# Gate-output units placed among the scores, numerators and norms of the exponential-gate mixer

## The chip, the cores and the metric

The kernel runs on one core of one Trainium2 chip. The metric is the device time of one execution in microseconds (us), the median over several runs. Engines: TensorE (PE; PEld is its weight load), VectorE (DVE), ScalarE (ACT), GpSimd (POOL); SyncE (SP) only issues DMAs.

## The reference

256 tokens of width 1024 go through four layers of a first block and one layer of a second. A first-block layer is a feed-forward (half added), a mixer (HGRN, the exponential-gate mixer, sliding-window attention, HGRN), a second feed-forward and a gated addition. Only layer 1's mixer, `mlstm_mixer`, is touched: four heads, queries and keys of 128, values of 256. It runs in chunks in the reference; the kernel computes the same in closed form over all 256 tokens:

```python
q, k, v, og = jnp.split(x @ w_qkvo, [dqk_all, 2 * dqk_all, 2 * dqk_all + D_MODEL], axis=-1)
...
scores = jnp.einsum('bhtk,bhsk->bhts', q_, k_) * w_intra
num = w_inter[..., None] * jnp.einsum('bhtk,bhkv->bhtv', q_, C) + jnp.einsum('bhts,bhsv->bhtv', scores, v_)
den = w_inter * jnp.einsum('bhtk,bhk->bht', q_, n) + jnp.sum(scores, axis=-1)
h = num / jnp.maximum(jnp.abs(den), jnp.exp(-m_t))[..., None]
...
h = rmsnorm(from_chunks(h), norm_g.reshape(ML_HEADS, ML_DV))
h = h.reshape(B, T, D_MODEL).astype(x.dtype) * jax.nn.sigmoid(og)
return h @ w_out
```

## The kernel before

All weights come as units of 1 MB (128 partitions x 2048 floats). Each unit passes four hands, in the order in which the phases consume the units: SyncE loads it into one of four `raw` buffers, ScalarE's `high` casts it to the coarse part `w_hi`, VectorE's `low` forms the rest, `w_lo`, and TensorE multiplies both with the two parts of the operand in 48 matmuls (`project`, `project_tokens`). There are three buffers of `w_hi` and `w_lo`, so `high(m)` waits until TensorE has finished unit m-3 (`weights_used`). Every engine has one program in a fixed order that is written by hand; semaphores hold it where another engine isn't ready. What stands behind a waiting instruction on its engine waits too.

The exponential-gate mixer (`ml`) has 16 units, called u0 to u15 here: u0 to u3 queries and keys, u4 to u7 values, u8 to u11 the output gate `og`, u12 to u15 the output projection (`w_out`). Before, TensorE does u0 to u7; then the gate columns and rows of heads (`cols`, `bcast`), the scores of four heads, the guard rows, for each head its numerators and its denominator, the square sums of the four heads (two blocks of 256 columns each, L1119 and L1120); then u8 to u11, and u12 to u15. VectorE in the meantime forms the arguments of the weights (L2323, L2324), masks them and multiplies them with the scores (L2328 to L2331), copies the numerators out of PSUM (L2335), forms the norm (L2339 to L2344), scales the heads with it (L2349), and then per gate unit, in `tail`: scale (L1919), low part of the operand (L2087), weights, product (L2097). ScalarE has exponentials, squares, logarithm and, in `gates_out`, per gate unit the sigmoid (L1507) and the coarse cast of the operand (L1509). The operand of u12 has four pairs of chunks, and `w_out` waits for each pair by itself (`mo_ready`), the fourth ahead of the last quarter of u12.

`ring` says how many PSUM banks the projections rotate over: 4 or 2; a unit waits until VectorE has read the bank's last content (`bank_read`). `besides` puts a block of other matmuls ahead of the given place within a unit. A place is one eighth of the unit: six matmuls. The HGRN mixers use both.

## Time and profile before

| | us |
|---|---|
| median of 3 runs | 2505.98 |
| lowest and highest | 2505.77, 2507.32 |
| profiled execution, first to last instruction | 2505.3 |
| TensorE busy in it | 2485.4 |
| VectorE busy in it | 1823.0 |
| ScalarE busy in it | 1294.7 |

The page of the profile describes one execution. The share of busy time of TensorE is 99%, but a matmul counts as busy while it waits for the array or runs at a lower clock, and the ends of matmuls are modelled: busy does not mean fast. The granted clock is given as a share of 2.4 GHz; 0.50 is 1.2 GHz. The mixer that is changed is passed once.

### The profile page before, as it was taken

Reading aid. Unit: us, or ns where it says so; the run is one execution under the profiler, and the core shown is the slowest. Engines: PE = TensorE matmul, PEld = TensorE weight load, DVE = VectorE, ACT = ScalarE, POOL = GpSimd, SP = SyncE. Lnnn points to the kernel's source line nnn. Section 1 sums busy time; section 2 is a strip of 40 time slices with the busy share of each in tenths; the row PEclk is TensorE's granted clock in tenths of the full one; section 3 lists DMA queues with packets and bytes.
Section 4 is the critical chain, followed back from the end, with each engine's and each line's share of the span. In section 5 each row is a group of like instructions: output and inputs, shape, how many; then the busy total and the mean of one; then the engine's idle time right before and its main releaser. Section 6 shows DMA issues by size and latency. Waiting matters only on the chain.

```text
span 2505.3 us, 41816 instructions
## 1 busy us (share of the span) xinstructions
PE 2485.4 (99%) x17552; PEld 2278.0 (91%) x17552; DVE 1823.0 (73%) x2203; ACT 1294.7 (52%) x1476; POOL 29.3 (1%) x62
## 2 busy tenths in 40 slices
PE   9999999999999999999999999999999999999999
PEld 8889998898898988988888889888999889999999
DVE  7857678677856777678567876785867868788755
ACT  5545365455534565465466554654535555444643
POOL 0000000000000000000000000000000000011000
PEclk9999999999999999999999999999999999999999
DMA  7554345554544355545543554455424554445352
GB/s 268 200 202 178 110 151 191 202 184 169 201 176 161 141 180 193 194 169 189 201 148 123 186 203 183 171 199 202 170 101 175 199 202 168 169 144 173 139 194 85
DMA packets 62270, 438.04 MB, mean 175 GB/s; under 512 B 7536, under 2 KB 7664, under 8 KB 10128
## 3 DMA queue, kind: packets, MB, share of 16 engines
q1 hardware_dynamic: 59472, 426.95, 47.1%
q0 software_dynamic: 2624, 8.52, 1.1%
q8 instruction: 139, 2.28, 0.4%
q14 instruction: 35, 0.29, 0.0%
HBM read 431.25 MB, written 1.05 MB: 173 GB/s over the span
## 4 chain that ended last, share of the span: by engine, by line
PE 92%; DVE 4%; ACT 2%; issue 1%; DMA 0%; SPq 0%; DVEq 0%; ACTq 0%
PE ps L756 19%; PE ps L838 13%; PE ps L851 12%; PE ps L869 11%; PE ps L840 7%; PE ps L857 6%; PE ps L774 6%; PE ps L870 5%; PE ps L790 2%; PE ps L872 1%; PE ps L873 1%; PE ps L874 1%; ACT w_hi L1395 1%; DVE w_lo L1857 1%; PE ps L938 1%
## 5 line engine op out<-in xcount | busy, mean ns | idle before, releaser
L1857 DVE TENSOR_TENSOR w_lo<-raw,w_hi 128x2048 fp32r<-128x2048 f32 x404 | 924.5, 2291 | 284.5 <-ACT w_hi L1395 275.5
L1395 ACT CAST w_hi<-raw 128x2048 fp32r<-128x2048 f32 x404 | 770.5, 1908 | 530.1 <-PE ps L870 214.3
L756 PE MATMUL ps<-right,w_hi 128*128 128x256 f32 x2112 | 391.3, 285 | 0.1
L756 PEld LDWEIGHTS ps<-right,w_hi 128*128 128x128 f32 x2112 | 332.2, 192 | 3.2 <-issue 1.7
L756 PE MATMUL ps<-right,w_lo 128*128 128x256 f32 x1056 | 298.7, 283 | 0.0
L869 PE MATMUL ps<-hidden,w_hi 128*128 128x512 f32 x768 | 269.3, 393 | 0.0
L838 PE MATMUL ps<-left,w_hi 128*128 128x512 f32 x736 | 256.7, 395 | 1.8 <-DVE left L1913 1.8
L838 PE MATMUL ps<-right,w_hi 128*128 128x512 f32 x736 | 256.7, 395 | 0.2 <-DVE right L2035 0.2
L1938 DVE TENSOR_TENSOR scratch<-ps,scratch 128x512 f32<-128x512 f32 x176 | 121.7, 691 | 155.7 <-ACT scratch L1431 155.7
L870 PE MATMUL ps<-hidden,w_lo 128*128 128x256 f32 x768 | 214.3, 279 | 0.0
L1448 ACT CAST hidden<-scratch 128x256 fp32r<-128x256 f32 x128 | 52.0, 406 | 300.8 <-DVE scratch L1946 300.8
L840 PE MATMUL ps<-right,w_lo 128*128 128x256 f32 x736 | 204.2, 278 | 0.0
L840 PE MATMUL ps<-left,w_lo 128*128 128x256 f32 x736 | 204.2, 278 | 0.0
L756 PEld LDWEIGHTS ps<-right,w_lo 128*128 128x128 f32 x1056 | 202.5, 192 | 0.3
L756 PE MATMUL ps<-left,w_hi 128*128 128x256 f32 x992 | 184.4, 285 | 0.1
L869 PEld LDWEIGHTS ps<-hidden,w_hi 128*128 128x128 f32 x768 | 143.9, 187 | 34.4
L838 PEld LDWEIGHTS ps<-left,w_hi 128*128 128x128 f32 x736 | 138.0, 188 | 34.6 <-issue 2.4
L838 PEld LDWEIGHTS ps<-right,w_hi 128*128 128x128 f32 x736 | 138.1, 188 | 32.8 <-DVE right L2035 0.8
L851 PE MATMUL ps<-left,w_hi 128*128 128x512 f32 x672 | 160.7, 391 | 0.0
L851 PE MATMUL ps<-right,w_hi 128*128 128x512 f32 x672 | 160.7, 391 | 0.0
L756 PEld LDWEIGHTS ps<-left,w_hi 128*128 128x128 f32 x992 | 156.1, 192 | 1.0 <-DVE w_lo L1857 0.3
L851 PEld LDWEIGHTS ps<-left,w_hi 128*128 128x128 f32 x672 | 123.6, 188 | 24.1
(356 smaller groups left out, 4499.2 us busy)
## 6 DMA issues: line engine op xcount, KB each, us to landing
raw<-weights_dram SPq DMA_DIRECT2D x404, 1024.0 KB, 4.8
scratch<-scratch POOLq DMA_DIRECT2D x48, 64.0 KB, 1.9
...
```

The costliest lines, as they stand in the source:

```text
L756: last = nc.tensor.matmul(bank(e, ring)[:, half * T:(half + 1) * T], l, r, start=(place == 0 and j == 0 and half == 0), stop=(place == KC ...
L774: last = nc.tensor.matmul(o[:, b * T:(b + 1) * T], l, r, start=(k == 0 and j == 0), stop=(k == KC - 1 and j == 2))
L838: nc.tensor.matmul(o, w_hi[:, w, wc], both(XG[2][:, k]), start=(k == 0), stop=False, skip_group_check=True)
L840: last = nc.tensor.matmul(o[:, T:2 * T], w_lo[:, w, wc], XG[0][:, k, :], start=False, stop=(k == KC - 1), skip_group_check=True)
L851: nc.tensor.matmul(ps[:, up_bank(i, j) + half, :], w_hi[:, w, wc], both(XG[2][:, k]), start=(k == 0), stop=False, skip_group_check=True)
L857: last = nc.tensor.matmul(ps[:, up_bank(i, j) + half, T:2 * T], w_lo[:, w, wc], XG[0][:, k, :], start=False, stop=(k == KC - 1), skip_grou ...
L869: nc.tensor.matmul(o, w_hi[:, w, wc], both(a), start=start, stop=False, skip_group_check=True)
L870: return nc.tensor.matmul(o[:, T:2 * T], w_lo[:, w, wc], a[:, 0], start=False, stop=True, skip_group_check=True)
L1395: nc.scalar.copy(w_hi[:, m % SPLIT, :], raw[:, m % RAW, :]).then_inc(weights_hi, 1)
L1448: nc.scalar.copy(hidden_parts(i, j)[:, 0], FFN_H[:, j % 2]).then_inc(hidden_hi, 1)
L1857: V.tensor_tensor(w_lo[:, m % SPLIT, :], raw[:, m % RAW, :], w_hi[:, m % SPLIT, :].bitcast(F32), ALU.subtract).then_inc(weights_split, 1)
L1938: V.tensor_tensor(FFN_T[j % 2], up_pair(i, j)[:, :, 0:T], FFN_SMALL, ALU.add).then_inc(bank_read, 1)
```

## The change

On TensorE the units u7 to u11 are no longer bare. Columns and rows stand ahead of place 1 of u7 and the scores ahead of place 4; numerators of heads 0 and 1 within u8; guards, the numerators of heads 2 and 3 and all denominators within u9; the square sums within u10. u4 to u11 rotate over two PSUM banks, since the others hold the blocks (`score_bank`, banks 2 and 3 for numerators). The two squared blocks of a head are added by VectorE (`sum_squares`, into `ML_SS`), and TensorE's square sums are two matmuls of 512 columns in place of eight of 256. VectorE masks a head's weights with one instruction in place of two. The code of `gates_out` and `tail` is gone, and the order on ScalarE and VectorE is written out: gates 0 to 2 are scaled as their units end, their sigmoids, products, casts and low parts stand behind the norm, each kind for all three; the fourth gate follows behind the weights of u13. Nothing else in the program is moved.

```diff
@@ -518,6 +518,7 @@
         ML_DEN = chunks(5 * UNIT + 1024, 4)
         ML_ROWS = chunks(6 * UNIT, 8)
         ML_T = chunks(0, KC)
+        ML_SS = chunks(14336, 4)
...
+        def score_bank(h):
+
+            return (ps[:, 2], ps[:, 3], ps[:, 4, P:512], ps[:, 5])[h][:, 0:384]
...
-                for u in range(4, 8):
-                    project_tokens(n0 + u, e0 + u, XG)
...
-                pe.wait_ge(m["ucol"], 1)
-                pe.wait_ge(m["arg"], ML_HEADS)
-                for h in range(ML_HEADS):
-                    last = nc.tensor.matmul(ps[:, 6 + h // 2, (h % 2) * T:(h % 2 + 1) * T], selector(h),
-                                            ML_ROWS[0:4, 7, :], start=True, stop=True)
-                last.then_inc(m["guard"], 1)
-                for h in range(ML_HEADS):
+
...
+                def guards():
+                    pe.wait_ge(m["ucol"], 1)
+                    pe.wait_ge(m["arg"], ML_HEADS)
+                    for h in range(ML_HEADS):
+                        last = nc.tensor.matmul(ps[:, 6 + h // 2, (h % 2) * T:(h % 2 + 1) * T], selector(h),
+                                                ML_ROWS[0:4, 7, :], start=True, stop=True)
+                    last.then_inc(m["guard"], 1)
+
+                def numerators(h):
                     pe.wait_ge(m["w"], h + 1)
+                    if h >= 2:
+                        pe.wait_ge(m["h"], h - 1)
                     w0, w1 = ML_W[:, h, 0:T], ML_W[:, h, T:T + P]
                     for d in range(2):
                         v = ML_V[:, :, h * ML_DV + d * P:h * ML_DV + (d + 1) * P]
-                        nc.tensor.matmul(ps[:, h, d * T:(d + 1) * T], v[:, 0], w0, start=True, stop=False,
+                        nc.tensor.matmul(ps[:, 2 + h % 2, d * T:(d + 1) * T], v[:, 0], w0, start=True, stop=False,
                                          skip_group_check=True)
-                        last = nc.tensor.matmul(ps[:, h, d * T + P:(d + 1) * T], v[:, 1], w1, start=False, stop=True,
-                                                skip_group_check=True)
+                        last = nc.tensor.matmul(ps[:, 2 + h % 2, d * T + P:(d + 1) * T], v[:, 1], w1, start=False,
+                                                stop=True, skip_group_check=True)
                     last.then_inc(m["num"], 1)
...
-                pe.wait_ge(m["gexp"], 1)
-                for h in range(ML_HEADS):
...
+                def denominators(p):
+                    pe.wait_ge(m["w"], 3 + p)
...
+                def pair_of_heads(p):
+                    numerators(2 + p)
+                    denominators(p)
+
+                def square_sums():
+                    pe.wait_ge(m["gexp"], 1)
+                    for p in range(2):
+                        pe.wait_ge(m["ss"], p + 1)
+                        nc.tensor.matmul(ps[:, 6 + p, :], ones, ML_SS[:, 2 * p:2 * p + 2].rearrange("p c t -> p (c t)"),
+                                         start=True, stop=True).then_inc(m["sums"], 1)
+                for u in range(4, 7):
+                    project_tokens(n0 + u, e0 + u, XG, ring=2)
+                project_tokens(n0 + 7, e0 + 7, XG, ring=2, besides={1: columns_and_rows, 4: scores})
+                project(n0 + 8, e0 + 8, XG, ring=2, besides={2: lambda: numerators(0), 4: lambda: numerators(1)})
+                project(n0 + 9, e0 + 9, XG, ring=2,
+                        besides={0: guards, 1: lambda: pair_of_heads(0), 3: lambda: pair_of_heads(1)})
+                project(n0 + 10, e0 + 10, XG, ring=2, besides={1: square_sums})
+                project(n0 + 11, e0 + 11, XG, ring=2)
                 pe.wait_ge(m["h"], ML_HEADS)
-                for u in range(8, 12):
-                    project(n0 + u, e0 + u, XG)
                 w_out(i, n0 + 12, e0 + 12)
...
                 for h in range(ML_HEADS):
                     act.wait_ge(m["arg"], h + 1)
                     nc.scalar.activation(ML_W[:, h], ML_W[:, h], ACT.Exp).then_inc(m["exp"], 1)
+                high(n0 + 7 + SPLIT)
+                square(0)
+                square(1)
+                high(n0 + 8 + SPLIT)
                 act.wait_ge(m["guard"], 1)
                 nc.scalar.activation(ML_GUARD.rearrange("p c t -> p (c t)"),
                                      ps[:, 6:8, :].rearrange("p b t -> p (b t)"), ACT.Exp).then_inc(m["gexp"], 1)
...
+                square(2)
+                square(3)
...
+                high(n0 + 9 + SPLIT)
                 act.wait_ge(m["nrm"], 2)
                 link(nc.scalar.activation(ML_GUARD, ML_GUARD, ACT.Ln))
                 for p in range(2):
                     r = ML_GUARD[:, 2 * p:2 * p + 2]
                     nc.scalar.activation(r, r, ACT.Exp, scale=-0.5).then_inc(m["rs"], 1)
-                gates_out(i, m, n0 + 8, e0 + 8, ML_T, ACT.Sigmoid)
+                for u in range(3):
+                    sigmoid(u)
+                for u in range(3):
+                    operand(u)
+                high(n0 + 10 + SPLIT)
+                sigmoid(3)
+                operand(3)
+                for u in range(11, 16):
+                    high(n0 + u + SPLIT)

...
+                def weights_of(h):
+                    blocks = ML_W[:, h].rearrange("p (b t) -> p b t", t=P)[:, 0:3:2]
                     dve.wait_ge(m["exp"], h + 1)
-                    V.tensor_tensor(ML_W[:, h, 0:P], ML_W[:, h, 0:P], causal, ALU.mult)
-                    link(V.tensor_tensor(ML_W[:, h, T:T + P], ML_W[:, h, T:T + P], causal, ALU.mult))
+                    link(V.tensor_tensor(blocks, blocks, causal.unsqueeze(1).broadcast_to([P, 2, P]), ALU.mult))
                     dve.wait_ge(m["scores"], h + 1)
-                    V.scalar_tensor_tensor(ML_W[:, h], ps[:, h, 0:384], ML_DQK ** -0.5, ML_W[:, h], ALU.mult,
+                    V.scalar_tensor_tensor(ML_W[:, h], score_bank(h), ML_DQK ** -0.5, ML_W[:, h], ALU.mult,
                                            ALU.mult).then_inc(m["w"], 1)
-                for h in range(ML_HEADS):
...
+                def sum_squares(p):
+                    dve.wait_ge(m["sq"], 2 * p + 2)
+                    two = ML_T[:, 4 * p:4 * p + 4].rearrange("p (h d) t -> p h d t", d=2)
+                    V.tensor_tensor(ML_SS[:, 2 * p:2 * p + 2], two[:, :, 0], two[:, :, 1], ALU.add).then_inc(m["ss"], 1)
...
+                def gate(u):
+                    scale(n0 + 8 + u, e0 + 8 + u, OUT[:, 2 * u:2 * u + 2], ring=2)
+
+                def product(u):
+                    dve.wait_ge(m["gate"], u + 1)
+                    V.tensor_tensor(OUT[:, 2 * u:2 * u + 2], ML_H[:, 2 * u:2 * u + 2], OUT[:, 2 * u:2 * u + 2],
+                                    ALU.mult).then_inc(m["prod"], 1)
...
+                def low_part(u):
+                    dve.wait_ge(mo_high, 4 * rcols(i) + u + 1)
...
+                weights_of(0)
+                weights_of(1)
+                values(7)
+                weights_of(2)
+                weights_of(3)
+                low(n0 + 7 + SPLIT)
+                take(0)
+                take(1)
+                gate(0)
+                low(n0 + 8 + SPLIT)
+                take(2)
+                take(3)
+                sum_squares(0)
+                sum_squares(1)
                 dve.wait_ge(m["gexp"], 2)
                 link(V.tensor_tensor(ML_DEN, ML_DEN, ML_GUARD, ALU.max))
                 link(V.scalar_tensor_tensor(ML_DEN, ML_DEN, EPS, ML_DEN, ALU.mult, ALU.mult))
+                gate(1)
+                low(n0 + 9 + SPLIT)
                 for p in range(2):
                     two = slice(2 * p, 2 * p + 2)
                     dve.wait_ge(m["sums"], p + 1)
                     V.scalar_tensor_tensor(ML_GUARD[:, two], pair(6 + p, True), 1.0 / ML_DV, ML_DEN[:, two], ALU.mult,
                                            ALU.add).then_inc(m["nrm"], 1)
+                gate(2)
                 dve.wait_ge(m["h"], ML_HEADS)
                 for c in range(KC):
                     dve.wait_ge(m["rs"], c // 4 + 1)
                     ins = V.scalar_tensor_tensor(ML_H[:, c], ML_H[:, c], gain(S_MLN, c), ML_GUARD[:, c // 2], ALU.mult,
                                                  ALU.mult)
                 link(ins)
-                tail(i, m, n0 + 8, e0 + 8, ML_T, ML_H)
+                for u in range(3):
+                    product(u)
+                for u in range(3):
+                    low_part(u)
+                low(n0 + 10 + SPLIT)
+                gate(3)
+                product(3)
+                low_part(3)
+                low(n0 + 11 + SPLIT)
+                residual(i, n0 + 12, e0 + 12)
```

On TensorE, before, behind the rows of heads (L1087): scores (L1092, L1093; the second line's rows repeat four times), guards (L1098), the first numerators (L1106, L1108).

```order
L1087 MATMUL ps<-scratch,common 128x256 x4
L1092 MATMUL ps<-scratch 128x256
L1093 MATMUL ps<-scratch 128x128
...
L1098 MATMUL ps<-scratch,common 128x256 x4
L1106 MATMUL ps<-scratch 128x256
L1108 MATMUL ps<-scratch 128x128
L1106 MATMUL ps<-scratch 128x256
L1108 MATMUL ps<-scratch 128x128
```

On TensorE, after, within u9: L761 is the matmul of `project`, L1108 the guards, L1119 and L1121 numerators, L1130 and L1131 denominators.

```order
L761 MATMUL ps<-right,w_hi 128x256
L1108 MATMUL ps<-scratch,common 128x256 x4
L761 MATMUL ps<-right,w_hi 128x256
L761 MATMUL ps<-right,w_lo 128x256
L761 MATMUL ps<-right,w_hi 128x256 x2
L761 MATMUL ps<-right,w_lo 128x256
L761 MATMUL ps<-right,w_hi 128x256
L1119 MATMUL ps<-scratch 128x256
L1121 MATMUL ps<-scratch 128x128
L1119 MATMUL ps<-scratch 128x256
L1121 MATMUL ps<-scratch 128x128
L1130 MATMUL ps<-scratch,common 128x256
L1131 MATMUL ps<-scratch,common 128x128
```

The guards had the scores directly ahead of them and now have all of u8, and each group of numerators has projections around it.

On VectorE, before, from the norm on: L2344 sums with the denominator, L2349 scaling of the heads, L1919 scale of a gate, L1857 `low`, L2097 product, L2087 low part of the operand.

```order
L2344 SCALAR_TENSOR_TENSOR scratch<-ps,scratch 128x512 x2
L2349 SCALAR_TENSOR_TENSOR scratch<-scratch,smalls 128x256 x8
L1919 TENSOR_TENSOR scratch<-ps,rstd 128x512
L1857 TENSOR_TENSOR w_lo<-raw,w_hi 128x2048
L2097 TENSOR_TENSOR scratch<-scratch 128x512
L1919 TENSOR_TENSOR scratch<-ps,rstd 128x512
L2087 TENSOR_TENSOR left<-scratch,left 128x2x256
L1857 TENSOR_TENSOR w_lo<-raw,w_hi 128x2048
L2097 TENSOR_TENSOR scratch<-scratch 128x512
L1919 TENSOR_TENSOR scratch<-ps,rstd 128x512
L2087 TENSOR_TENSOR left<-scratch,left 128x2x256
L1857 TENSOR_TENSOR w_lo<-raw,w_hi 128x2048
```

On VectorE, after, from the scale of gate 1 on: L1956 scale of a gate, L1894 `low` (of u12, then u13), L2398 sums, L2404 scaling of the heads, L2369 products, L2374 low parts of the operand.

```order
L1956 TENSOR_TENSOR scratch<-ps,rstd 128x512
L1894 TENSOR_TENSOR w_lo<-raw,w_hi 128x2048
L2398 SCALAR_TENSOR_TENSOR scratch<-ps,scratch 128x512 x2
L1956 TENSOR_TENSOR scratch<-ps,rstd 128x512
L2404 SCALAR_TENSOR_TENSOR scratch<-scratch,smalls 128x256 x8
L2369 TENSOR_TENSOR scratch<-scratch 128x512 x3
L2374 TENSOR_TENSOR left<-scratch,left 128x2x256 x3
L1894 TENSOR_TENSOR w_lo<-raw,w_hi 128x2048
L1956 TENSOR_TENSOR scratch<-ps,rstd 128x512
L2369 TENSOR_TENSOR scratch<-scratch 128x512
L2374 TENSOR_TENSOR left<-scratch,left 128x2x256
L1894 TENSOR_TENSOR w_lo<-raw,w_hi 128x2048
```

The first low part of the operand stood behind one product; it now stands behind three, and the scale and product of the fourth gate stand behind u13's weights.

On ScalarE, before: L1626 logarithm, L1629 the two exponentials, L1395 `high`, L1507 sigmoid, L1509 cast of the operand.

```order
L1626 ACTIVATE scratch<-scratch 128x1024
L1629 ACT_TABLE_LOAD
L1629 ACTIVATE scratch<-scratch 128x512 x2
L1395 CAST w_hi<-raw 128x2048
L1507 ACT_TABLE_LOAD
L1507 ACTIVATE scratch<-scratch 128x512
L1509 CAST left<-scratch 128x2x256
L1395 CAST w_hi<-raw 128x2048
L1507 ACTIVATE scratch<-scratch 128x512
L1509 CAST left<-scratch 128x2x256
L1395 CAST w_hi<-raw 128x2048
L1507 ACTIVATE scratch<-scratch 128x512
```

On ScalarE, after: L1422 `high` (u12), L1655 logarithm, L1658 exponentials, L1633 sigmoid, L1637 cast of the operand, L1422 again (u13).

```order
L1422 CAST w_hi<-raw 128x2048
L1655 ACT_TABLE_LOAD
L1655 ACTIVATE scratch<-scratch 128x1024
L1658 ACT_TABLE_LOAD
L1658 ACTIVATE scratch<-scratch 128x512 x2
L1633 ACT_TABLE_LOAD
L1633 ACTIVATE scratch<-scratch 128x512 x3
L1637 CAST left<-scratch 128x2x256 x3
L1422 CAST w_hi<-raw 128x2048
L1633 ACTIVATE scratch<-scratch 128x512
L1637 CAST left<-scratch 128x2x256
```

The cast of u13's weights now stands behind three casts of the operand, and the fourth sigmoid and cast behind it.

## Rows read from the trace of the kernel before

**Rows 1.** The page, part 4: the chain that ended last, shares by engine.

```profile
PE 92%; DVE 4%; ACT 2%; issue 1%; DMA 0%; SPq 0%; DVEq 0%; ACTq 0%
```

**Rows 2.** Waits, TensorE: line, waited for: us in total, times, longest us.

```profile
PE ps L1013 <- DVE scratch L2182: 2.5, 4, 0.6
PE ps L1098 <- DVE scratch L2324: 2.1, 1, 2.1
PE ps L838 <- DVE left L1913: 1.8, 2, 1.0
```

**Rows 3.** Windows: us, busy time and count by engine, PEclk, DMA share, GB/s.

```profile
803.00:803.50 0.50, 0.50 (x3) 0.45 (x2) 0.47 (x3) 0.00 (x0) 0.00 (x0) 0.79 0.78 328
803.50:804.00 0.50, 0.50 (x2) 0.33 (x2) 0.50 (x2) 0.00 (x0) 0.00 (x0) 0.50 0.01 0
...
810.00:810.50 0.50, 0.50 (x4) 0.45 (x3) 0.00 (x0) 0.00 (x0) 0.00 (x0) 0.88 0.00 0
```

**Rows 4.** Timeline, TensorE: start us, us, line, operation, xcount, idle before it.

```profile
794.74 0.60 PE L1083 MATMUL ps<-common,scratch 4*128 4x4 f32 x4
...
802.08 2.57 PE L1098 MATMUL ps<-scratch,common 4*128 4x256 f32 x8 [2.08 <-DVE scratch L2324]
...
811.30 0.60 PE L1106 MATMUL ps<-scratch 128*128 128x256 f32 x2
...
813.26 0.60 PE L1106 MATMUL ps<-scratch 128*128 128x256 f32 x2
...
815.23 0.60 PE L1119 MATMUL ps<-scratch,common 128*128 128x256 f32 x2
...
818.25 0.59 PE L1120 MATMUL ps<-scratch,common 128*128 128x256 f32 x2
...
841.71 0.28 PE L756 MATMUL ps<-left,w_hi 128*128 128x256 f32 x1
```

**Rows 5.** Timeline, ScalarE, same columns; L1395 is the cast of a unit's weights.

```profile
820.91 1.06 ACT L1626 ACTIVATE scratch<-scratch 128x1024 f32<-128x1024 f32 x1 [2.57 <-DVE scratch L2344]
...
823.28 1.16 ACT L1629 ACTIVATE scratch<-scratch 128x512 f32<-128x512 f32 x2
...
842.63 0.63 ACT L1507 ACTIVATE scratch<-scratch 128x512 f32<-128x512 f32 x1 [0.39 <-DVE scratch L1919]
...
844.03 0.62 ACT L1509 CAST left<-scratch 128x512 fp32r<-128x512 f32 x1 [0.76 <-DVE scratch L2097]
...
847.72 1.91 ACT L1395 CAST w_hi<-raw 128x2048 fp32r<-128x2048 f32 x1 [1.27 <-PE ps L756]
...
853.48 1.91 ACT L1395 CAST w_hi<-raw 128x2048 fp32r<-128x2048 f32 x1 [3.85 <-PE ps L756]
```

**Rows 6.** Timeline, TensorE, an HGRN stage (308 us) and the attention stage.

```profile
308.16 1.89 PE L1047 MATMUL ps<-scratch,common 128*128 128x256 f32 x8
...
310.01 0.28 PE L756 MATMUL ps<-left,w_lo 128*128 128x256 f32 x1
...
1287.93 2.74 PE L1220 MATMUL ps<-scratch,common 128*128 128x512 f32 x6
```

**Rows 7.** Timeline, VectorE, of the mixer.

```profile
789.61 0.41 DVE L2316 SCALAR_TENSOR_TENSOR scratch<-scratch 4x256 f32<-4x256 f32 x1
...
819.59 1.29 DVE L2344 SCALAR_TENSOR_TENSOR scratch<-ps,scratch 128x512 f32<-128x512 f32 x2
...
824.03 3.26 DVE L2349 SCALAR_TENSOR_TENSOR scratch<-scratch,smalls 128x256 f32<-128x256 f32 x8 [3.15 <-ACT scratch L1629]
...
833.31 2.29 DVE L1857 TENSOR_TENSOR w_lo<-raw,w_hi 128x2048 fp32r<-128x2048 f32 x1 [1.12 <-ACT w_hi L1395]
...
843.30 0.69 DVE L2097 TENSOR_TENSOR scratch<-scratch 128x512 f32<-128x512 f32 x1
...
844.68 0.69 DVE L2087 TENSOR_TENSOR left<-scratch,left 128x512 fp32r<-128x512 f32 x1 [0.69 <-ACT left L1509]
```

**Rows 8.** One window of an HGRN stage with a wait of L1013.

```profile
265.00:270.00 5.00, 4.39 (x83) 4.07 (x82) 5.00 (x7) 0.00 (x0) 0.00 (x0) 1.00 0.59 213
```

108 lines of the change are left out of this document (44 added, 64 removed).

## The prediction, made before the changed kernel ran

> Units of weights of the mixer are called u0 to u15 here, and times inside the stage are those of the trace of before, also where they are worked out for the changed kernel: up to u7 the two programs do the same.
>
> **What bounds it now.** First the chain that ended last, on the page: 92% of it is TensorE [rows 1], so time comes only from work taken off TensorE or from waits taken off it. Then the waits of TensorE, sorted by their total: the first line is four waits of up to 0.6 us in the HGRN stages, the second is a single one of 2.1 us, the longest of the whole span, of L1098 for VectorE's arguments (L2324) [rows 2]. It is in the stage that is changed. Then the clock there: half-microsecond windows show it at 1.00 (2.4 GHz), 0.79 in the window from 803.0, 0.50 (1.2 GHz) from 803.5, and 0.88 in the one from 810.0 [rows 3]. Read as a share of each window at the lower level, that is a fall at 803.3 and a rise at 810.1: 6.8 us at 1.2 GHz, begun 3.4 us after the engine had run out of work at 800.0. Last the timeline of TensorE, for what each block of this stage costs at 2.4 GHz [rows 4]; the 800.0 is its 802.08 less the 2.08 us of idle time in that row.
>
> **What the stage costs now.** A unit is 5.75 us, 0.12 a matmul, as two casts that follow two ends of units show (847.72 and 853.48) [rows 5]. So u7 begins at 794.74 - 5.75 = 789.0, and u12, begun at 841.71, ends at 847.5 [rows 4]: 58.5 us for u7 to u12 with all that lies between.
>
> **What TensorE has to do afterwards.** Six units 34.5. Columns, rows and scores, now 794.74 to 800.0, 5.3: of it 2.6 are the scores' sixteen passes, and a gap or two goes; I take 5.1, of which 2.4 stand ahead of the scores. Guards: eight passes of 256 columns at 0.21 us (fourteen such passes stand between 815.23 and 818.25), 1.7. A head's numerators and denominators at 2.4 GHz: 811.30 to 813.26, 1.96; four make 7.8 [rows 4]. Square sums: now sixteen passes of 256 columns, from 815.23 to 818.25 and two more, 3.4; with the two blocks of a head added by VectorE, four passes of 512 columns. Six such passes of L1220 span 2.74, the last one with its 0.59: 0.43 each [rows 6], so 1.7. Sum 34.5 + 5.1 + 1.7 + 7.8 + 1.7 = 50.8. Without any wait and at 2.4 GHz the change gives 58.5 - 50.8 = **7.7 us**: 2.1 the wait, 1.7 the square sums, 3.4 half of the 6.8 us at 1.2 GHz, 0.5 gaps between the blocks. That blocks of another kind stand between projections costs nothing by itself: eight passes of L1047, put between two matmuls of L756 in an HGRN stage, take 308.16 to 310.01 with the first matmul behind them, 1.85, and eight at 0.21 with one at 0.12 are 1.83 [rows 6]. At worst it is the 0.1 us of a gap at each of eight places, 0.8.
>
> **Who is late afterwards.** TensorE's work is now closer together, but VectorE and ScalarE have the same chain, and it must be walked. An operation is followed on its engine by the next after its duration less 0.09 us; from ScalarE to VectorE and back a result takes 0.03 us, as 844.03 + 0.62 and then 844.68 show [rows 5, 7]; to and from TensorE I take 0.1.
>
> In u7 the columns stand after a quarter of the first half (789.7), and wait for L2316's row, ready at 790.02 [rows 7]: **0.35 us** new wait. u7 then ends at 800.1 (790.1 + 2.4 + 18 matmuls 2.15 + scores 2.6 + 24 matmuls 2.9). The weights of heads 0 and 1 are done by 798.0 and those of 2 and 3, behind the values of u7, by 803.0; numerators 0 stand at 801.5, numerators 2 at 810.9, guards at 808.4: no wait. What hides these is u7 and u8 themselves, with 3 to 12 us in hand; without that cover a wait like the old one, 2 us, would be back. Two PSUM banks for u4 to u11 cost nothing as long as a unit is read before the next but one starts, and VectorE reads it within 1 us of its end, or 5 us ahead. Masking with one instruction and the two additions of squares (0.69 each, as L2097 [rows 7]) lie in VectorE's idle time. SyncE's loads are released by VectorE's low parts, four units ahead of use as before, and none of these is delayed by more than the 3 us in which u13 to u15 still have theirs. u8 ends at 808.4 (5.75 and two numerators of 1.28), u9 at 821.0 (5.75, guards 1.7, 4 x 1.28), u10 at 828.5 (5.75 + 1.7; VectorE has the sums of squares by 818.4, 3.4 us ahead of their place), u11 at 834.2.
>
> Now the tail, which feeds u12, the first unit of the output projection. The cast of u12's weights starts at u9's end, 821.2, takes 1.9, VectorE's low part 2.29: 825.4. Two L2344 (1.29) to 826.6. Ln 1.06, the table load that fills 821.97 to 823.28, half of the 1.16 of the two exponentials: 829.7. Eight L2349, 3.26 us, to 832.9 [rows 5, 7]. Then the order shown above decides: three products (0.69 each) before the first low part, which ends at 835.5. TensorE has been free since 834.2: **a wait of 1.4 us**. In u12 each pair of chunks is 1.44 us, so the fourth pair is wanted at 835.6 + 4.3 = 840.0. It is made thus: ScalarE's cast of u13's weights from 835.5 to 837.4, VectorE's low part of them to 839.7, and only behind it the scale of gate 3, although u11 ended at 834.2; sigmoid 841.0, product 841.7, cast 842.4, low part 843.1, at TensorE 843.2: **a wait of 3.2 us**. Queued behind these are only low parts of u14 and the residual, which have 4 us in hand. The old order had the same last links (842.63, 843.30, 844.03, 844.68) [rows 5, 7], but there u11 ended at 841.7 and the fourth pair was wanted at 846.0; there was 0.6 us left. So the stall goes to the output projection: 0.35 + 1.4 + 3.2 = 5.0 us are given back, and 7.7 - 5.0 = 2.7 us stay. No matter how early TensorE gets there, u12 cannot end before 843.2 + 1.4 = 844.6, against 847.5.
>
> **The clock after the new wait.** Waits of 1.0 us (L838) and 0.6 us (L1013) stand in the list [rows 2] and the 5 us around one of L1013's show 1.00 [rows 8]; that of 2.08 us was followed by the fall. One of 3.2 us is not shown. A price from both sides: nothing, or 6.8 us at half speed, 3.4. Since a part may fall in the wait itself (3.2 us is long) or a unit's passes may lose a little less than half, I take 2.7. The 3.2 us are nearer to the 2.08 than to the 1.0, so I take the fall as happening. Sum: -7.7 + 5.0 + 2.7 = 0.0. The sum is made against the profiled execution, whose span is 2505.3; the median of the three runs is 2505.98, 0.7 above it, and I carry that over: the forecast is **2506.0 us**.
>
> **Rivals.**
> - The waits come, but the clock stays at 2.4 GHz (1.4 and 3.2 us with 4.3 us of work between). For it: a wait of 1.0 us is followed by work at full speed, and the 3.2 us stand between stretches of solid work, while the old wait had blocks with operands of four rows on both sides. Against it: the length. 2506.0 - 2.7 = 2503.3. Chance 0.25.
> - The operand is not late, because the tail's links come earlier than I walked them. The whole gain, 2506.0 - 7.7 = 2498.3; it counts as faster by over 0.2% if at least 2.3 of the 5.0 us of waits are missing and the clock holds. For it: nothing in the rows but that a sum of some fifteen links can be off. Against it: each link has its own row. Chance 0.15.
> - Slower: the small blocks between projections make the clock fall again and again. TensorE now changes kind of work eight times in 40 us. Each fall costs up to 3.4; from 2506.0 - 2.7 it takes three of them to pass +5.0 (7.5 above), and four give 2506.0 - 2.7 + 13.6 = 2516.9. Against it: the HGRN stages are built this way, have waits of their own, and the 5 us around such a wait stand at 1.00 [rows 8]. Chance 0.06. The Trainium skill, page "TensorE: Matmul & The Clock Gate", section "A second HAM failure mode: psum-queue depth-cycling", states this rule: frequent short idles between groups of matmuls that cycle through PSUM banks make the clock swing between half and full. By that rule this change would be slower; the trace of the HGRN stage does not agree with it here.
> - The wait moves into u7 or u8 instead: the values of u7, between the weights of heads 1 and 2 on VectorE, hold these back until u7's end. They are 8 us early by my times, so it would need an error of that size; with a fall there too the end is near 2507. Chance 0.04.
>
> **How the numbers follow.** Forecast 0.50. About 0.2% (5.0 us) can be told from no change with this kernel. Faster by more than that: the second rival and a sliver of the first, 0.17. Slower: the third and a little of the forecast's upper end, 0.07. Within: 0.76. The range holds the forecast (2505.3 to 2506.7 by the bounds 2.0 and 3.4 of the clock, and 1 us for the runs' own spread), the first rival, the fourth, and of the second the part in which only half of the waits are missing: 2500.2 to 2508.5; the rest of the second and the third are left out.
>
> **What would show it.** Right: L1098's wait gone and the matmul line of the guards without idle time; the new square-sum line with four passes of some 0.6 us; waits of TensorE for the left operand's low part, 1.4 and 3.2 us, at the start and before the fourth pair of u12; a stretch of 0.50 granted clock in u12 or u13 in place of that at 803.3. Wrong: if gate 3's scale on VectorE starts within 1 us of u11's end, or the list of waits has no such line, the walk of the tail is wrong; if a clock below 1.00 stands in u7 to u11, the third rival is at work; if no stretch is below 1.00, the first.

## The result and the profile after

| | before | after |
|---|---|---|
| median of 20 runs each, us | 2506.06 | 2509.57 |
| lowest and highest | 2505.4, 2507.64 | 2508.4, 2510.52 |
| profiled execution, first to last instruction | 2505.3 | 2508.4 |
| the same execution's own time | 2507.32 | 2510.39 |

The ratio is 1.0013, 95% interval 1.0007 to 1.0019: 3.5 us slower, inside the 0.2% that was called no change, but 1.1 us above the predicted range. Medians here and below are over fast runs; one run, of the version with the tail reordered, took 6251.58 us and is not counted.

The page of after shows almost nothing. Its first part has TensorE busy for 0.1 us more than before and no higher share:

```profile
PE 2485.5 (99%) x17540; PEld 2277.4 (91%) x17540; DVE 1823.4 (73%) x2201; ACT 1294.6 (52%) x1476; POOL 29.3 (1%) x62
```

The waits of TensorE in after (line, waited for: us in total, times, longest) answer to [rows 2]. L1098's 2.1 us are gone, and another line stands first: L761 (`project`) for the low part of the left operand, L2374. The 0.3 us of L1088, the columns, are in the list of the window from 785 us.

```profile
PE ps L761 <- DVE left L2374: 4.3, 2, 2.9
PE ps L1018 <- DVE scratch L2199: 2.5, 4, 0.6
...
PE ps L1088 <- DVE scratch L2336: 0.3, 1, 0.3
```

The timeline of TensorE in after (start us, us, line, operation, idle before it) has the blocks and the waits at their places. It answers to [rows 4]:

```profile
790.22 0.60 PE L1088 MATMUL ps<-common,scratch 4*128 4x4 f32 x4 [0.29 <-DVE scratch L2336]
790.69 1.97 PE L1092 MATMUL ps<-scratch,common 4*128 4x256 f32 x8
792.59 0.51 PE L779 MATMUL ps<-w_hi,right 128*128 128x256 f32 x1
792.90 0.42 PE L779 MATMUL ps<-w_lo,right 128*128 128x256 f32 x1
...
810.28 1.99 PE L1108 MATMUL ps<-scratch,common 4*128 4x256 f32 x8
812.20 0.39 PE L761 MATMUL ps<-right,w_hi 128*128 128x256 f32 x1
...
825.66 1.88 PE L1142 MATMUL ps<-scratch,common 128*128 128x512 f32 x4
...
839.71 0.36 PE L761 MATMUL ps<-left,w_hi 128*128 128x256 f32 x1 [1.37 <-DVE left L2374]
...
847.17 0.48 PE L761 MATMUL ps<-left,w_hi 128*128 128x256 f32 x1 [2.92 <-DVE left L2374]
```

No wait stands at the guards (L1108), the square sums are four passes, and u12 begins 1.37 us late and its fourth pair 2.92 us late. VectorE's timeline shows why the fourth pair is late, as the order on it says: u13's weights (L1894) at 841.46, and only then gate 3's scale (L1956), product (L2369) and low part (L2374). It answers to [rows 7]:

```profile
841.46 2.29 DVE L1894 TENSOR_TENSOR w_lo<-raw,w_hi 128x2048 fp32r<-128x2048 f32 x1 [0.69 <-ACT w_hi L1422]
843.67 0.68 DVE L1956 TENSOR_TENSOR scratch<-ps,rstd 128x512 f32<-128x512 f32 x1
845.04 0.69 DVE L2369 TENSOR_TENSOR scratch<-scratch 128x512 f32<-128x512 f32 x1 [0.69 <-ACT scratch L1633]
846.42 0.69 DVE L2374 TENSOR_TENSOR left<-scratch,left 128x512 fp32r<-128x512 f32 x1 [0.68 <-ACT left L1637]
```

What was not foreseen is in the windows of after (busy time and count by engine, PEclk, DMA share, GB/s), which answer to [rows 3]:

```profile
792.50:793.00 0.50, 0.50 (x3) 0.41 (x3) 0.50 (x1) 0.01 (x1) 0.00 (x0) 0.70 0.00 0
793.00:793.50 0.50, 0.50 (x4) 0.50 (x4) 0.50 (x2) 0.00 (x0) 0.00 (x0) 0.50 0.00 0
...
796.00:796.50 0.50, 0.50 (x5) 0.50 (x5) 0.50 (x3) 0.38 (x2) 0.00 (x0) 0.89 1.10 459
...
813.00:813.50 0.50, 0.50 (x4) 0.42 (x3) 0.50 (x1) 0.34 (x1) 0.00 (x0) 0.68 0.00 0
...
816.50:817.00 0.50, 0.50 (x4) 0.47 (x4) 0.00 (x0) 0.50 (x1) 0.00 (x0) 0.91 0.69 262
...
847.00:847.50 0.50, 0.33 (x2) 0.34 (x3) 0.11 (x1) 0.50 (x1) 0.00 (x0) 0.81 1.04 442
...
850.50:851.00 0.50, 0.50 (x5) 0.50 (x5) 0.50 (x2) 0.50 (x1) 0.00 (x0) 0.78 0.00 0
```

Read as before, as a share of each window at the lower level, these are three stretches at 0.50: 792.70 to 796.11, 813.18 to 816.59 and 847.31 to 850.72, 3.41 us each and 10.23 together, where before had 6.83. The last begins at the end of the wait of 2.92 us. The first two have no wait of more than 0.29 us ahead of them. Each begins within 1 us of the end of a block whose matmuls have 4 rows in place of 128 (`4*128` in the timeline): the rows of heads and the guards. TensorE's busy share is full in them, so no busy column and no wait tells of it; the count of matmuls does, if like is compared with like: projections alone make six or seven in half a microsecond at 1.00 and four or five in the first stretch, numerators and denominators five at 1.00 and three or four in the second.

**The stage as a measure.** Each unit's end starts a weight cast on ScalarE, so the casts give the time from the end of u6 to the end of u15 without modelled ends: 867.73 - 789.30 = 78.43 us in after, 865.00 - 789.15 = 75.85 in before.

```profile
867.73 1.91 ACT L1422 CAST w_hi<-raw 128x2048 fp32r<-128x2048 f32 x1 [3.84 <-PE ps L761]
```

The difference, 2.6 us, is most of the 3.1 between the spans. The casts also price the three stretches, against versions that have the same blocks and no stretch there: u7 took 12.79 us in after and 11.29 in the version with the tail reordered, u9 14.75 and 13.10, and what follows u9 up to u15's end 42.53 in after and 41.03 in the version with 128 rows. So a stretch of 3.4 us cost 1.50 us in u7, 1.65 in u9 and 1.50 in the tail, 4.65 together. Half of 3.41 would be 1.7; projections lose less than half, since their matmuls follow each other after 0.12 us at 1.00 and after 0.21 at 0.50. The table under the experiments gives this stage for each kernel, together with the time at 0.50 in it.

### The profile page after: what moved, and what is told of

Same layout as the page of the kernel before. It is cut to its first block, busy times and chain, and to the rows that moved or that the text cites. A ratio compares the mean times of both kernels' runs of the same rounds, so it can differ in the third digit from the quotient of the medians.

```text
span 2508.4 us, 41793 instructions
## 1 busy us (share of the span) xinstructions
PE 2485.5 (99%) x17540; PEld 2277.4 (91%) x17540; DVE 1823.4 (73%) x2201; ACT 1294.6 (52%) x1476; POOL 29.3 (1%) x62
## 4 chain that ended last, share of the span: by engine, by line
PE 91%; DVE 5%; ACT 3%; issue 1%; DMA 0%; SPq 0%; DVEq 0%; ACTq 0%
PE ps L761 18%; PE ps L843 13%; PE ps L856 12%; PE ps L874 11%; PE ps L845 7%; PE ps L862 6%; PE ps L875 5%; PE ps L779 5%; PE ps L795 2%; DVE w_lo L1894 1%; ACT w_hi L1422 1%; PE ps L877 1%; PE ps L878 1%; PE ps L879 1%; PE ps L943 1%
## 5 line engine op out<-in xcount | busy, mean ns | idle before, releaser
L1894 DVE TENSOR_TENSOR w_lo<-raw,w_hi 128x2048 fp32r<-128x2048 f32 x404 | 924.4, 2290 | 285.0 <-ACT w_hi L1422 275.9
L1422 ACT CAST w_hi<-raw 128x2048 fp32r<-128x2048 f32 x404 | 770.4, 1907 | 537.0 <-PE ps L875 214.8
L761 PE MATMUL ps<-right,w_hi 128*128 128x256 f32 x2112 | 392.8, 285 | 0.1
L761 PEld LDWEIGHTS ps<-right,w_hi 128*128 128x128 f32 x2112 | 332.6, 192 | 3.8 <-issue 2.2
L761 PE MATMUL ps<-right,w_lo 128*128 128x256 f32 x1056 | 298.7, 283 | 0.0
L761 PEld LDWEIGHTS ps<-right,w_lo 128*128 128x128 f32 x1056 | 202.5, 192 | 0.5 <-issue 0.2
L761 PE MATMUL ps<-left,w_hi 128*128 128x256 f32 x992 | 186.1, 287 | 4.4 <-DVE left L2374 4.3
L843 PEld LDWEIGHTS ps<-left,w_hi 128*128 128x128 f32 x736 | 138.0, 188 | 34.9 <-issue 2.6
L843 PEld LDWEIGHTS ps<-right,w_hi 128*128 128x128 f32 x736 | 138.1, 188 | 32.8 <-DVE right L2072 0.8
L761 PEld LDWEIGHTS ps<-left,w_hi 128*128 128x128 f32 x992 | 157.4, 193 | 5.6 <-DVE left L2374 3.1
L856 PEld LDWEIGHTS ps<-right,w_hi 128*128 128x128 f32 x672 | 123.6, 188 | 24.2
```

What stands on the lines that cost most here:

```text
L761: last = nc.tensor.matmul(bank(e, ring)[:, half * T:(half + 1) * T], l, r, start=(place == 0 and j == 0 and half == 0), stop=(place == KC ...
L843: nc.tensor.matmul(o, w_hi[:, w, wc], both(XG[2][:, k]), start=(k == 0), stop=False, skip_group_check=True)
L856: nc.tensor.matmul(ps[:, up_bank(i, j) + half, :], w_hi[:, w, wc], both(XG[2][:, k]), start=(k == 0), stop=False, skip_group_check=True)
L1422: nc.scalar.copy(w_hi[:, m % SPLIT, :], raw[:, m % RAW, :]).then_inc(weights_hi, 1)
L1894: V.tensor_tensor(w_lo[:, m % SPLIT, :], raw[:, m % RAW, :], w_hi[:, m % SPLIT, :].bitcast(F32), ALU.subtract).then_inc(weights_split, 1)
```

## The experiments

Theory: the change's own gain and waits are as walked, and the excess is the clock, which falls behind blocks of 4 rows as well as behind the wait in the tail. Rivals: the small blocks between projections make it fall whatever their shape; only the tail's wait matters; the falls are random.

| kernel | median us | ratio to before, 95% | stage us | at 0.50, us |
|---|---|---|---|---|
| before | 2506.06 | | 75.85 | 6.83 |
| after | 2509.57 | 1.0013 [1.0007, 1.0019] | 78.43 | 10.23 |
| after, 128 rows in both | 2506.11 | 1.0003 [0.9994, 1.0012] | 73.26 | 0 |
| after, tail reordered | 2506.03 | 1.0000 [0.9991, 1.0009] | 72.52 | 0 |
| both edits | 2503.62 | 0.9990 [0.9981, 0.9998] | 72.02 | 0 |
| both, cast earlier | 2502.08 | 0.9984 [0.9975, 0.9993] | 70.82 | 0 |
| before, 128 rows | 2504.93 | 0.9994 [0.9986, 1.0003] | 74.06 | 3.42 |
| after, square sums undone | 2509.49 | 1.0016 [1.0007, 1.0025] | 77.99 | 6.82 |
| before, 4-row block added | 2512.15 | 1.0025 [1.0015, 1.0035] | 81.03 | 13.65 |
| before, 128-row block added | 2510.16 | 1.0016 [1.0007, 1.0025] | 79.32 | 6.83 |
| after again | 2509.14 | 1.0009 [1.0000, 1.0018] | 78.34 | 10.24 |
| before again | 2505.72 | 1.0001 [0.9992, 1.0010] | 74.22 | 6.83 |
| after, guards 128 rows | 2508.16 | 1.0007 [0.9998, 1.0016] | 76.01 | 6.83 |
| after, rows 128 rows | 2507.12 | 1.0004 [0.9995, 1.0013] | 76.70 | 6.83 |

Medians are over 9 to 20 runs. Stage and 0.50 are those of the one profiled execution, which need not be the median one. The ratio is to runs of before that were taken together with the kernel's own; their medians went from 2505.49 to 2506.78. Some paragraphs use a run's mean clock, which is on record for every run, to three digits. The last part of the program is at 0.50 in nearly every profile, for up to 2.7 us of the span. So 1.000 (less than 2.5 us at 0.50 in the whole run) excludes a stretch of 3.4 us, 0.998 or less (over 7.5 us) means at least one, and 0.999 tells nothing.

**The blocks over 128 rows.** What the rows beyond the four contribute is zero, so the matmuls compute the same.

```diff
-            return common[0:ML_HEADS, (6 + h) * P:(7 + h) * P]
+            return common[:, (6 + h) * P:(7 + h) * P]
...
-                                                ML_ROWS[0:4, 6, :], start=True, stop=True)
+                                                ML_ROWS[:, 6, :], start=True, stop=True)
...
-                                                ML_ROWS[0:4, 7, :], start=True, stop=True)
+                                                ML_ROWS[:, 7, :], start=True, stop=True)
```

> The changed kernel, with the rows of heads and the guards (two blocks of four matmuls of 256 columns) multiplied over all 128 rows of the array in place of 4: the selector's other rows are zero, so the result is the same. Theory (few rows): the clock falls in u7 and in u9 because these blocks use 4 of 128 rows, not because small blocks stand between projections. Then no window of u7 to u9 is below 1.00, the fall in u12 stays, and the time falls by two stretches of 3.4 us at half clock, 1.5 to 1.7 us each: about 2506.4 us, ratio to the kernel before 1.000. Rival (small blocks and changes of kind): all blocks stand where they stood, so both falls stay and the time is 2509.6, ratio 1.0014.

The median is 2506.11 us (2504.89 to 2507.75). The windows of this kernel where after had its three stretches:

```profile
792.50:796.50 4.00, 4.00 (x31) 3.84 (x31) 3.93 (x12) 1.97 (x4) 0.00 (x0) 1.00 0.48 160
812.50:816.50 4.00, 4.00 (x29) 3.82 (x28) 1.08 (x3) 0.63 (x1) 0.00 (x0) 1.00 0.59 215
843.00:847.00 4.00, 3.77 (x31) 3.77 (x32) 2.89 (x3) 3.17 (x2) 0.00 (x0) 1.00 0.28 113
```

and the first two of these windows of after:

```profile
792.50:796.50 4.00, 4.00 (x20) 3.91 (x20) 3.96 (x11) 1.71 (x5) 0.00 (x0) 0.57 0.44 129
812.50:816.50 4.00, 4.00 (x18) 3.45 (x17) 2.86 (x2) 0.95 (x2) 0.00 (x0) 0.58 0.14 16
```

The first of these windows is 4.00 us busy in both kernels, with 31 matmuls in one and 20 in the other. The blocks, their places, the banks and the waits are the same, and the eight passes of a block take about the same time:

```profile
790.49 1.99 PE L1092 MATMUL ps<-scratch,common 128*128 128x256 f32 x8
...
808.32 1.89 PE L1108 MATMUL ps<-scratch,common 128*128 128x256 f32 x8
809.86 0.47 PE L761 MATMUL ps<-right,w_hi 128*128 128x256 f32 x1
```

What differs besides the rows are the two ends of a block. The next projection starts 1.54 us after the guards over 128 rows (808.32 to 809.86) and 1.92 after those over 4 (810.28 to 812.20 in after), both at 1.00. The casts of two versions without any stretch agree: u9 takes 13.10 us with the guards over 4 rows (tail reordered) and 12.70 over 128 (both edits), u7 11.29 and 11.17. So few rows cost 0.5 us in this stage that has nothing to do with the clock.

It is not the small blocks as such that make the clock fall. The Trainium skill, page "TensorE: Matmul & The Clock Gate", section "A second HAM failure mode: psum-queue depth-cycling", puts a swinging clock down to frequent short idles between groups of matmuls that cycle through PSUM banks. This kernel keeps groups and banks and stands at 1.00 in this execution, so the banks are not what lowers the clock in after. The short idles of the rule are not excluded by it, since the stop of some 0.3 us behind a block of 4 rows goes with the rows. Against them speaks that the waits of 0.3 and 1.4 us in this same execution have no stretch behind them.

The fall in u12, which was expected to stay, is not there either: this execution has no fall at all and the same waits as after. Its stage is 73.26, 2.59 under that of before, where the walk said 2.7. The kernel's other runs go up to 2.9 us higher, so the tail's wait is probably followed by a fall in some of them; their mean clocks are 0.999, which does not tell, but for 0.998 in the longest.

**The tail reordered.** On VectorE u13's weights go behind the gate, and the pairs are finished one by one. On ScalarE gate 3's sigmoid and cast stand ahead of u13's cast (not shown below).

```diff
...
-                link(ins)
-                for u in range(3):
-                    product(u)
-                for u in range(3):
-                    low_part(u)
-                low(n0 + 10 + SPLIT)
-                gate(3)
-                product(3)
-                low_part(3)
...
+                scaled_heads(0, 1, 2, 3, 4, 5)
+                product(0)
+                product(1)
+                low_part(0)
+                scaled_heads(6, 7)
+                product(2)
+                low_part(1)
+                gate(3)
+                low_part(2)
+                product(3)
+                low_part(3)
+                low(n0 + 10 + SPLIT)
                 low(n0 + 11 + SPLIT)
```

> The changed kernel with another order behind the norm: the first low part of the operand behind six of the eight scalings and two products, the fourth gate's scale, product and low part ahead of u13's low part, and u13's cast behind the fourth sigmoid and cast. Theory (order of the tail): the two waits of 1.4 and 2.9 us and the fall behind them go; instead u13 waits up to 1.2 us for its low part. 2509.6 - 4.3 - 1.5 + 1.2 = 2505.0, ratio 0.9996. Rival (the chain itself is too long, the order hardly matters): the operand is still 3 us or more late in u12, 2508 or more.

Measured 2506.03 us (2504.79 to 2507.57), 1.0 above the forecast. The two waits of 4.3 us together have shrunk to three of 0.8 in all, and u13 now waits 1.7 for its low part, where 1.2 was expected. Its profiled execution, the fastest, has no stretch below 1.00 in the mixer though both 4-row blocks stand in it. The four longest runs, 1.6 to 2.8 us higher, have a mean clock of 0.998 against 1.0, so falls occur in these.

**Both.**

> Both edits together: 128 rows for the two blocks, and the other order behind the norm. If the theories hold and add up: 2509.6 - 3.1 - 4.6 = 2501.9 us, ratio 0.9983, no window of the mixer below 1.00. If the small blocks are what lowers the clock: 2505.0.

Measured 2503.62 us, between the two forecasts: 1.7 above the theory's 2501.9 and 1.4 under the rival's 2505.0. The clock part of the theory held, with no stretch in the mixer. What it had too high is the order of the tail: in executions without a fall, reordering takes only 1.2 us off the stage (73.26 with 128 rows alone, 72.02 with both), where 3.1 were counted (4.3 - 1.2). All runs lie within 1.2 us (2502.81 to 2503.97) with a mean clock of 0.999 or 1.0. The waits of L761 in this kernel's mixer:

```profile
PE ps L761 <- DVE w_lo L1893: 1.7, 1, 1.7
PE ps L761 <- DVE left L2373: 0.8, 3, 0.4
```

Each edit alone takes 3.5 us off after's 2509.57, both together 6.0. With both, the spread of the runs shrinks as well. That fits a clock that falls in some executions and not in others: take away what makes it fall, and the runs agree.

**u13's cast earlier**, on top of both: the cast of the operand is split around it.

```diff
-                for u in range(3):
-                    operand(u)
+                operand(0)
+                operand(1)
+                high(n0 + 10 + SPLIT)
+                operand(2)
                 sigmoid(3)
                 operand(3)
-                for u in range(10, 16):
+                for u in range(11, 16):
```

> The wide rows and the reordered tail together, and u13's cast moved on ScalarE from behind the second cast of the gate's operands to the place between the 2nd and the 3rd, with gate 3's sigmoid behind it. Theory (with no fall of the clock left, what remains of the tail is u13's wait of 1.7 us for its low part, that hangs on its cast): the wait shrinks to about 0.6 us, and the time is 1.1 us under the version with both edits, about 2502.5 us. Rival (that wait is set by VectorE's own order, not by the cast): the wait stays at 1.7 us and the time at 2503.6 us.

Measured 2502.08 us (2501.55 to 2502.67), 0.4 under the forecast, and no run of it overlaps one of the version without it. ScalarE's timeline has the cast in what was idle time, 833.71:

```profile
832.66 1.15 ACT L1637 CAST left<-scratch 128x512 fp32r<-128x512 f32 x2
833.71 1.90 ACT L1422 CAST w_hi<-raw 128x2048 fp32r<-128x2048 f32 x1
835.54 0.62 ACT L1637 CAST left<-scratch 128x512 fp32r<-128x512 f32 x1
```

and TensorE's waits for u13's low part are 0.5 in place of 1.7:

```profile
PE ps L761 <- DVE left L2375: 0.8, 3, 0.4
...
PE ps L761 <- DVE w_lo L1895: 0.5, 1, 0.5
```

Its stage is 70.82, 5.0 under that of before. This is the version that beats both kernels, against before by 0.9984 [0.9975, 0.9993].

**Before with 128 rows**: the same edit of shapes in the kernel before.

> The kernel before, with the rows of heads and the guards over 128 rows; its wait of 2.08 us stays. If the wait alone makes the clock fall there: unchanged, 2506.1, ratio 1.000, still 0.50 from about 803. If the guards' 4 rows behind the wait have their part in it: no fall, 3 us less, 2503, ratio 0.9988.

Measured 2504.93 us (2503.45 to 2505.72), between the two forecasts of 2506.1 and 2503. The wait of 2.2 us stays, with one stretch of 3.42 us (801.88 to 805.30) in the profiled execution:

```profile
802.00:802.50 0.50, 0.50 (x2) 0.41 (x3) 0.47 (x2) 0.27 (x1) 0.00 (x0) 0.50 1.08 459
```

Three of the eleven runs have a mean clock of 1.0, at 2503.45 to 2504.19, and so no such stretch. So a wait of 2.2 us alone can be followed by a fall, and is not always. As far as one profile shows, the wait has its share in before's 6.8 us, and the rows have theirs.

**Square sums as eight matmuls of 256 columns, sixteen passes** (the additions by VectorE stay, their result is not used):

```diff
-                        nc.tensor.matmul(ps[:, 6 + p, :], ones, ML_SS[:, 2 * p:2 * p + 2].rearrange("p c t -> p (c t)"),
-                                         start=True, stop=True).then_inc(m["sums"], 1)
+                        for h in (2 * p, 2 * p + 1):
+                            o = ps[:, 6 + p, (h % 2) * T:(h % 2 + 1) * T]
+                            nc.tensor.matmul(o, ones, ML_T[:, 2 * h], start=True, stop=False)
+                            last = nc.tensor.matmul(o, ones, ML_T[:, 2 * h + 1], start=False, stop=True)
+                        last.then_inc(m["sums"], 1)
```

> The changed kernel with the square sums as eight matmuls of 256 columns again (VectorE's additions stay, their result is not used by TensorE). Both theories: sixteen passes of 0.21 us in place of four of 0.43 in u10, 1.7 us more work, all of which delays u10's end and with it the tail: 2511.3 us. If the clock or the tail absorbs it: 2509.6.

The forecast of 2511.3 us was too high: measured are 2509.49, with after at 2509.57. The first wait of the tail shrinks from 1.4 to 0.8 us, since TensorE comes to it later. The other 1.1 us are set off in this execution by 1.7 us less lost to the clock (6.82 at 0.50 in place of 10.23), and the medians do not show them. What is saved ahead of a wait that another engine ends is not saved: that took 0.6 of the square sums' 1.7 us.

**The price of few rows by itself**: eight matmuls of 256 columns (sixteen passes) more in the middle of u9 of before, over 4 rows and over 128 rows. Their result is not used.

```diff
+                def extra():
+                    pe.wait_ge(m["nrm"], 2)
+                    for _ in range(8):
+                        nc.tensor.matmul(ps[:, 5, 0:T], common[0:ML_HEADS, 6 * P:7 * P], ML_ROWS[0:4, 6, :], start=True, stop=True)
...
-                    project(n0 + u, e0 + u, XG)
+                    project(n0 + u, e0 + u, XG, besides={4: extra} if u == 9 else {})
```

> The kernel before, with eight more matmuls of 256 columns in the middle of u9, amid solid projections, over 4 rows of the array (their result goes to an unused bank). No wait and no PSUM rotation. Theory (few rows): 3.4 us of work and a fall of the clock behind it or within it, 1.5 us or more: 2506.1 + 3.4 + 1.5 = 2511.0 or more. Rival (only waits or many small blocks lower the clock): 2509.5, clock 1.00 in u9 and u10.

> The same eight matmuls at the same place over all 128 rows. Both theories: 3.4 us more, 2509.5, and the clock at 1.00 in u9 and u10. Its difference to the run with 4 rows is the price of few rows.

Measured 2512.15 us (2509.18 to 2514.34) and 2510.16 (2508.89 to 2511.05), the latter 0.7 above its forecast. With 128 rows the stage grows by the block's own work and nothing else, 79.32 - 75.85 = 3.5 us. With 4 rows the median is 2.0 us higher still, though the ranges overlap; some 0.4 of it is an estimate for the two ends of the block, by the guards above, and the rest is left for the clock. The block of 4 rows in its timeline, and windows behind it:

```profile
826.20 3.99 PE L1127 MATMUL ps<-scratch,common 4*128 4x256 f32 x16
```

```profile
829.00:829.50 0.50, 0.50 (x4) 0.44 (x3) 0.50 (x2) 0.00 (x0) 0.00 (x0) 1.00 0.00 0
829.50:836.00 6.50, 6.50 (x29) 5.89 (x29) 0.46 (x2) 0.92 (x2) 0.00 (x0) 0.50 0.47 164
836.00:836.50 0.50, 0.50 (x5) 0.50 (x4) 0.50 (x2) 0.50 (x1) 0.00 (x0) 0.67 0.00 0
```

and the block over 128 rows, with a window around it:

```profile
827.43 3.62 PE L1127 MATMUL ps<-scratch,common 128*128 128x256 f32 x16
```

```profile
827.00:836.00 9.00, 9.00 (x64) 8.58 (x64) 5.23 (x8) 4.26 (x5) 0.00 (x0) 1.00 0.33 118
```

Nothing waits at this place in either, and the only difference in the programs is the rows. From 829.5, still within the 4-row block's row, on the clock is at 0.50 for 6.8 us; behind the other it stays at 1.00.

**One block at a time.** The guards alone over 128 rows, and the rows of heads alone:

> The changed kernel with the guards alone over 128 rows (those beyond the four are zero in one operand); the rows of heads keep 4. Theory (each block of 4 rows is followed by its own stretch at half the clock, and so is the tail wait of 2.9 us): stretches at 0.50 near 793 us and near 847.5 us, none near 813 us; time 1.7 us under the changed kernel, about 2507.6 us. Rival (one block of 4 rows suffices, and the second stretch is an echo of the first): the stretch near 813 us stays, and the time at 2509.4 us.

> The changed kernel with the rows of heads alone over 128 rows; the guards keep 4 (and so do the eight narrow columns of 4 ahead of the rows). Theory: a stretch at 0.50 near 813 us and one near 847.5 us, none near 793 us; about 2507.6 us. Rival (the echo): neither near 793 nor near 813 us, since the first is gone; about 2505.9 us.

Rows alone: as the theory said, with one stretch behind the guards (810.76 to 814.18) and one that begins as the tail's wait ends (844.90 to 848.31), none near 793; 2507.12 us, 0.5 under the forecast.

```profile
793.00:793.50 0.50, 0.50 (x7) 0.50 (x6) 0.46 (x3) 0.00 (x0) 0.00 (x0) 1.00 0.00 0
...
812.00:812.50 0.50, 0.50 (x4) 0.44 (x3) 0.50 (x1) 0.00 (x0) 0.00 (x0) 0.50 0.00 0
...
846.00:846.50 0.50, 0.50 (x4) 0.50 (x4) 0.31 (x1) 0.16 (x1) 0.00 (x0) 0.50 0.28 98
```

That disproves the echo, since the second stretch came without a first. Guards alone: nothing near 813, but against the theory nothing near 793 either, where the 4-row block still stands. The tail instead has 6.8 us at 0.50, from within its second wait (842.44) on; 2508.16 us, 0.6 above the forecast.

```profile
790.00:796.00 6.00, 6.00 (x39) 5.38 (x40) 5.69 (x13) 3.72 (x5) 0.00 (x0) 1.00 0.57 201
810.00:816.00 6.00, 6.00 (x43) 5.66 (x42) 2.89 (x2) 2.07 (x3) 0.00 (x0) 1.00 0.30 93
842.00:842.50 0.50, 0.00 (x0) 0.00 (x0) 0.00 (x0) 0.50 (x2) 0.00 (x0) 0.94 1.08 459
...
843.00:849.00 6.00, 5.72 (x27) 5.72 (x27) 4.86 (x8) 3.20 (x2) 0.00 (x0) 0.50 0.37 135
```

So a block of 4 rows isn't always followed by a fall.

**The two kernels again**, for a second profile each.

> The changed kernel unchanged, for a second profile. Theory (falls of the clock behind blocks of 4 rows and behind the tail wait): about 2509.6 us, stretches at 0.50 of 3.4 us each, two to four of them, each of them beginning within 4 us behind a block of 4 rows (rows and columns in u7, guards in u10, and those of the other heads) or behind one of u12's two waits; waits of 1.4, 2.9 and 0.3 us as before. Rival (the falls come at random, whatever the matmuls): stretches also begin at places that have neither ahead of them.

> The kernel before, unchanged, for a second profile. Theory (the two levels of its times, near 2505.3 and 2507.2 us, differ by one stretch of 3.4 us at half the clock): if the profiled execution is near 2505.3 us (a span near 2503.4 us), it has 3.4 us at 0.50 behind the 2.1 us wait in place of 6.8 us; if it is near 2507.2 us, 6.8 us again. Rival (the levels differ elsewhere in the program): 6.8 us in either.

After: 2509.14 us, with stretches at 792.92, 813.40 and 847.53, within 0.3 us of their old places and none elsewhere in the mixer, as the theory said. Before: the theory's number missed and the rival's held. The profiled run was one of the low ones (2505.38), and still has 6.83 us at 0.50. The levels do not differ elsewhere in the program, though, but by where these stretches lie: 797.68 to 801.10, in the scores, and 804.51 to 807.92. The windows:

```profile
797.50:798.00 0.50, 0.50 (x4) 0.47 (x3) 0.50 (x1) 0.50 (x1) 0.00 (x0) 0.68 0.48 197
798.00:801.00 3.00, 3.00 (x11) 2.56 (x10) 2.96 (x8) 0.96 (x3) 0.00 (x0) 0.50 0.17 41
```

and the wait, which answers to the second line of [rows 2]:

```profile
PE ps L1098 <- DVE scratch L2324: 0.4, 1, 0.4
```

The first stretch lies in the scores and makes TensorE later at the guards, so the wait for VectorE shrinks from 2.1 to 0.4 us: a fall ahead of a wait costs nothing. In these two executions that, and not a missing stretch, separates 2505.38 from 2507.32 us (the stages differ by 1.6 us). The twenty runs of before lie in two groups, 2505.40 to 2506.13 and 2506.87 to 2507.64; whether this is what parts the groups was not profiled further. It also shows that before too has a fall that begins behind a 4-row block, ahead of any wait.

**The count over all profiled executions of after and its variants** with the blocks in u7 and u9 (after and after again, 128 rows, tail reordered, both, cast earlier, square sums undone, guards or rows wide): behind a block of 4 rows 6 of 10 were followed by a stretch at 0.50 (not both of the reordered tail, one of the undone square sums, the rows in the version with wide guards). Behind a block over 128 rows it was 0 of 8. The tail's wait of 2.9 us had a stretch that began within it or behind it in 5 of 6, the reordered tail in 0 of 3. In before and its variants the rows of heads stand ahead of any wait as well: there it was 2 of 4 over 4 rows (not before itself, nor the one with the 128-row block added) and 0 of 1 over 128.

## Why the prediction was wrong, point by point

- **TensorE's work without waits.** The stage came out in the version without falls 2.59 us under before, against 2.7. Removed, as said: the 2.1 us of wait and half of the square sums. With 4 rows, though, the blocks take 0.5 us more than the 0.21 us a pass that they were priced at, by what happens at their ends; that price was read from passes over 128 rows. The version without falls has its blocks over 128 rows and so does not show this.
- **The walk of the tail.** Right: 0.29, 1.37 and 2.92 us against 0.35, 1.4 and 3.2, for the reasons given, the order on VectorE above all. From the end of u9 to the operand's fourth pair it counted 22.0 us, and after has 21.97 (825.20 to 847.17). Its remedy confirms it: with the order changed, 4.3 us of waits became 0.8, plus 1.7 for u13.
- **The clock: the step that failed.** The prediction took before's 3.4 us (half of 6.8 at 1.2 GHz) as removed with the wait and put back one fall of 2.7 behind the new wait. After has three stretches, 10.23 us at 0.50, which cost 4.65 us by the casts: 1.95 more than the term of 2.7. The one in u12 and u13 that it forecast is among them and cost 1.50; the two in u7 and u9, 3.15 us, were put at nothing. With the 0.5 us of the blocks' ends and the 0.1 by which the version without falls missed the walk, 0.0 + 1.95 + 0.5 + 0.1 = 2.55, and the stage measured 2.58. The error lies in reading the stretch at 803.3 as caused by the wait alone. It stood behind two blocks of 4 rows as well, one of them behind the wait; with these over 128 rows 3.4 us at 0.50 were left of the 6.8. The change keeps the blocks and sets them apart, each in front of work that is on the path.
- **The cover that went.** Where before had a fall behind the first 4-row block (its second profile, not its first), it ran into the wait for VectorE and cost little. After, nothing waits there, so u7 pays in full, 1.50 us.
- **The rival of the repeated falls** had the right sign and the wrong cause, and 0.06 was too little. It held the number of small blocks responsible. The three versions in which both blocks use 128 rows have the same number, and no stretch in their profiles. And it was weighed against an HGRN stage at 1.00. That stage's blocks have `128*128` in their rows [rows 6], and those of this mixer `4*128` [rows 4]: the difference was in sight and not used. Its price per fall was too high as well: a fall lasts 3.4 us in after and costs 1.50 to 1.65, where 3.4 was charged.
- **The carry from span to median.** +0.7 was added. Each run's own time is 2.0 us above its span, so before's profiled execution was the one at 2507.32, 1.3 above the median. The 0.7 holds only if after's profiled execution stands as high in its runs; it stood 0.8 above its median, so half a microsecond of the miss in medians is this. Another 0.5 lies outside the stage: the spans differ by 3.1 us, the stages by 2.6.
- **Other rivals.** The clock that holds, the operand in time, and the wait in u7 or u8 did not happen.

What stays open: whether the few rows themselves or the short stops at the two ends of such a block make the clock fall, since every experiment changed both together; why only 6 of 10 such blocks are followed by a fall; how much of the 3.5 us between after and its 128-row version comes from fewer falls in the tail (that version's other runs weren't profiled); and whether 32 or 64 rows would do. This wasn't tried.
